# Two memory projections between the last turns of the query and key items of a hybrid decoder step

## The reference, cut to what matters

```python
z = rms_norm(h) @ w_in                     # conv group B, C, h; q, k, v; indexer queries and key
q, k = rope(rms_norm(q)), rope(rms_norm(k))
sel = top_k(indexer_scores(qi, iw, ki))    # 256 keys per prompt token, 66 per sample token
att = softmax(q @ k[sel]) @ v[sel]
h  += concat(B * conv3(C * h), att) @ w_out
mk, mv = split(rms_norm(mem_prompt, g_mem_src) @ w_kv_mem)   # 256 memory rows; mk is normed per head
h  += softmax(q_mem @ mk) @ mv @ w_o_mem
h  += ffn(h)
```

## Time and profile before

| | |
|---|---|
| median of 3 runs | 1862.89 us (1860.01 to 1864.6) |
| profiled execution, its own time | 1859.77 us |
| its span | 1858.0 us |
| mean granted TensorE clock | 0.954 |
| first key item on PE | 379.5 us |
| last turn of a key item | 452.5 us |
| scores of sample 0 | 462.1 us |
| prompt attention starts | 574.3 us |

### The profile page before, as it was taken

How to read it: one execution, slowest core, us unless ns; L and a number is a source line. 1 busy time by engine, 2 the same in 40 slices (tenths; PEclk the granted TensorE clock), 3 DMA queues, 4 the chain that set the end, 5 groups by cost and what they waited for, 6 DMA issues and landing times.

```text
span 1858.0 us, 33731 instructions
## 1 busy us (share of the span) xinstructions
PE 1719.4 (93%) x13725; PEld 1192.3 (64%) x13803; DVE 1113.3 (60%) x1901; ACT 810.9 (44%) x1475; POOL 735.1 (40%) x705
## 2 busy tenths in 40 slices
PE   6999999996787889989979997999999999999998
PEld 4543445443454655444568544888888888898998
DVE  5865665786797865456655237878888787300000
ACT  5465578744544864432355316544444444110100
POOL 3132266886540210320033416666666666401200
PEclk9998999997887999999978998999999999999999
DMA  7031112022424110301254112112121122321211
GB/s 229 17 104 51 35 35 85 30 74 90 155 76 137 53 47 1 111 1 35 89 155 140 62 40 91 46 53 63 46 69 47 47 69 86 97 95 39 94 36 29
DMA packets 136548, 132.75 MB, mean 71 GB/s; under 512 B 15358, under 2 KB 109630, under 8 KB 136356
## 3 DMA queue, kind: packets, MB, share of 16 engines
q1 hardware_dynamic: 123850, 118.79, 20.7%
q10 hardware_dynamic: 12544, 11.80, 2.0%
HBM read 114.58 MB, written 15.98 MB: 70 GB/s over the span
## 4 chain that ended last, share of the span: by engine, by line
PE 69%; DVE 15%; ACT 6%; issue 4%; POOL 3%; DMA 2%; SPq 1%; ACTq 0%; DVEq 0%; POOLq 0%
PE PS L1542 23%; PE PS L1599 5%; PE PS L1601 5%; PE PS L1600 5%; PE PS L938 4%; PE PS L939 4%; PE PS L940 4%; ACT arena L1674 2%; ACT arena L1615 2%; PE PS L1099 2%; PE PS L1097 2%; PE PS L1098 2%; PE PS L1244 1%; PE PS L1256 1%; POOL arena L2942 1%
## 5 line engine op out<-in xcount | busy, mean ns | idle before, releaser
L1542 PE MATMUL PS<-arena 128*128 128x272 f16 (+1 forms) x3696 | 430.6, 280 | 5.3 <-issue 5.3
L1542 PEld LDWEIGHTS PS<-arena 128*128 128x128 f16 (+1 forms) x3696 | 362.5, 98 | 73.4 <-issue 5.5
L1615 ACT ACTIVATE arena<-PS 128x512 f16<-128x512 f32 (+13 forms) x380 | 189.6, 530 | 229.4 <-PE PS L940 79.8
L1615 ACT ACTIVATE arena<-arena 128x512 f16<-128x512 f32 (+5 forms) x214 | 136.1, 657 | 235.9 <-PE PS L1542 116.4
L938 PE MATMUL PS<-arena 128*128 128x512 f16 (+3 forms) x648 | 227.9, 361 | 6.7 <-POOL arena L367 2.6
L367 POOL TENSOR_TENSOR arena<-arena 128x512 bf16<-128x512 f32 (+2 forms) x144 | 159.5, 1143 | 184.7 <-ACT arena L358 184.4
L939 PE MATMUL PS<-arena 128*128 128x512 f16 (+3 forms) x648 | 227.6, 361 | 0.0
L1599 PE MATMUL PS<-arena 128*128 128x256 f16 (+1 forms) x792 | 216.0, 273 | 1.4 <-POOL arena L916 1.0
L1601 PE MATMUL PS<-arena 128*128 128x256 bf16 (+1 forms) x792 | 215.9, 273 | 0.0
L1600 PE MATMUL PS<-arena 128*128 128x256 f16 (+1 forms) x792 | 215.9, 273 | 0.0
L940 PE MATMUL PS<-arena 128*128 128x512 bf16 (+2 forms) x609 | 212.6, 360 | 0.0
(11 more groups left out here) (351 smaller groups left out, 3713.7 us busy)
## 6 DMA issues: line engine op xcount, KB each, us to landing
arena<-w_gu SPq DMA_DIRECT2D x44, 512.0 KB, 4.8
arena<-w_down SPq DMA_DIRECT2D x8, 1408.0 KB, 7.6
arena<-w_in SPq DMA_DIRECT2D x8, 1024.0 KB, 5.5
arena<-w_kv_mem SPq DMA_DIRECT2D x8, 1024.0 KB, 5.3
arena<-cache_mem_k SPq DMA_DIRECT2D x32, 256.0 KB, 3.5
arena<-cache_mem_v ACTq DMA_DIRECT2D x28, 256.0 KB, 4.0
arena<-w_in SPq DMA_DIRECT2D x24, 256.0 KB, 3.9
arena<-x_prompt SPq DMA_DIRECT2D x9, 512.0 KB, 7.4
```

Source lines behind the costliest of these rows:

```text
L1542: mm = e.matmul(PS[:, product_bank(f, i) + c, 0:TC], w[:, i, k], s[i][:, q, c, :], start=first, stop=last)
L1615: e.activation(out, in_, ACT.Copy, **kw).then_inc(sem(name), 1)
```

## The change

Projections 0 and 1 of the memory leave the loop over samples and go between the last turns of the items: `memory_part(0, 0, 4)` behind the projection of item 35, then `(0, 4, 8)`, `(1, 0, 5)` and `(1, 5, 8)` in the three iterations after it, each in front of a turn. Projections 2 to 7 run one iteration sooner, `memory_part(b + 1)` in iterations 1 to 6. For that the row tiles are turned and split in items 27 and 31 in place of 29 and 35 (DVE's low parts behind items 28 and 32, before 30 and 37), chunk 1 is loaded behind the sixth key store, POOL splits it in front of the first value page (the other chunks stay where they were), the transposes of the conv state move from bank 7 to bank 5 and in front of the last turn, ACT evacuates projection b in iteration b, POOL's memset of `qm_all` moves behind the last rotation, and DVE's last update in the item loop from item 34 to item 35.

```diff
@@ sync @@
             B.load(e, 0)
-            store_roped(A_K)
+            store_roped(A_K, range(6))
             B.load(e, 1)
+            store_roped(A_K, range(6, NT))
@@ tensor @@
+            def memory_part(it, first, end):
...
             for L in range(NI1, NI + TURN_LAG):
-                if L == NI1 + 11:
+                if L == NI1 + 9:
                     NM.pe_turn(e, 0, lambda j: memx[:, j, :])
-                if L == NI1 + 17:
+                if L == NI1 + 13:
                     e.wait_ge(sem("nm_lo"), upto("nm_lo", 1))
                     NM.pe_turn(e, 1, lambda j: memx[:, j, :])
...
                 if L < NI:
                     project_item(L)
+                if L == NI - 1:
+                    e.wait_ge(sem("nm_lo"), upto("nm_lo", 2))
+                    memory_part(0, 0, 4)
+                if L == NI:
+                    memory_part(0, 4, KT)
+                if L == NI + 1:
+                    memory_part(1, 0, 5)
+                if L == NI + 2:
+                    e.wait_ge(sem("s2_raw"), NI)
+                    e.wait_ge(sem("s2_gn"), upto("s2_gn", 2 * NT))
+                    e.wait_ge(sem("conv_lo"), NC_T)
+                    for f in range(NC_T):
+                        t = e.transpose(PS[0:18, 5, f * P:(f + 1) * P], u_state[:, f, :], ident[:, :])
+                    t.then_inc(sem("mixst_tp"), 1)
+                    memory_part(1, 5, KT)
                 if L - TURN_LAG >= NI1:
                     turn_item(L - TURN_LAG)
...
             for b in range(DEC_B + 2):
+                part = 1 <= b < DEC_B - 1
                 if b < DEC_B:
-                    memory_part(b, 0, 3 if b else 5)
+                    if part:
+                        memory_part(b + 1, 0, 3)
...
-                    memory_part(b, 3 if b else 5, 6)
+                    if part:
+                        memory_part(b + 1, 3, 6)
                 if 1 <= b <= DEC_B:
                     sample_turn_probs(b - 1)
-                if b < DEC_B:
-                    memory_part(b, 6, KT)
+                if part:
+                    memory_part(b + 1, 6, KT)
@@ scalar @@
-                if L in (NI1 + 11, NI1 + 18):
-                    NM.act_hi(e, int(L == NI1 + 18))
+                if L in (NI1 + 9, NI1 + 13):
+                    NM.act_hi(e, int(L == NI1 + 13))
...
+            memory_out(0)
             for b in range(DEC_B + 1):
-                if b >= 1:
-                    memory_out(b - 1)
+                if 1 <= b < DEC_B:
+                    memory_out(b)
@@ vector @@
-                    if (L - NI1) % 2 == 0 and NI1 < L < NI - 1:
+                    if (L - NI1) % 2 == 0 and NI1 < L < NI - 2 or L == NI - 1:
                         update()
...
-                if L in (NI1 + 12, NI1 + 19):
-                    NM.dve_lo(e, int(L == NI1 + 19))
+                if L in (NI1 + 10, NI1 + 14):
+                    NM.dve_lo(e, int(L == NI1 + 14))
@@ gpsimd @@
-                if L == NI - 1:
-
-                    e.wait_ge(sem("s2_mm"), NI)
-                    e.memset(qm_all[:, :], 0.0).then_inc(sem("q_ht"), 1)
...
+            e.wait_ge(sem("s2_mm"), NI)
+            e.memset(qm_all[:, :], 0.0).then_inc(sem("q_ht"), 1)
...
+            e.wait_ge(sem("q_ht"), 5)
+            B.split_lo(e, 1)
             for b in range(DEC_B):
...
-                if b in (0, 2, 4):
+                if b in (2, 4):
                     B.split_lo(e, b // 2 + 1)
```

More of the change, by code:

```diff
@@ L1100, in _ @@
                 mm.then_inc(sem("s4_mm"), 1)
+            def memory_part(it, first, end):
+                c, j = it // 2, it % 2
+                if first == 0:
+                    if j == 0:
+                        B.ready(e, B_KV + c)
+                    if it >= 2:
+                        e.wait_ge(sem("mkv_ev"), it - 1)
+                out, wh, wl = PS[:, 6 + it % 2, :], B.high(c), B.low(c)
+                for k in range(first, end):
+                    e.matmul(out, xm_hi[j][:, k, :], wh[:, k, :], start=(k == 0), stop=False)
+                    e.matmul(out, xm_lo[j][:, k, :], wh[:, k, :], start=False, stop=False)
+                    mm = e.matmul(out, xm_hi[j][:, k, :], wl[:, k, :], start=False, stop=(k == KT - 1))
+                if end == KT:
+                    mm.then_inc(sem("mkv_mm"), 1)
             for L in range(NI1, NI + TURN_LAG):
-                if L == NI1 + 11:
+                if L == NI1 + 9:
                     NM.pe_turn(e, 0, lambda j: memx[:, j, :])
-                if L == NI1 + 17:
+                if L == NI1 + 13:
                     e.wait_ge(sem("nm_lo"), upto("nm_lo", 1))
@@ L1115, in _ @@
                     project_item(L)
+                if L == NI - 1:
[13 more added lines that the diff above has]
+                    memory_part(1, 5, KT)
                 if L - TURN_LAG >= NI1:
                     turn_item(L - TURN_LAG)
-            e.wait_ge(sem("s2_raw"), NI)
-            e.wait_ge(sem("s2_gn"), upto("s2_gn", 2 * NT))
-            e.wait_ge(sem("nm_lo"), upto("nm_lo", 2))
             e.wait_ge(sem("s4_ev"), len(L4))
@@ L1124, in _ @@
             e.wait_ge(sem("s2_lo"), split_items(NI))
[L1125 to L1128, removed]
             def sample_scores(b):
@@ L1160, in sample_values @@
                 e.wait_ge(sem("sv_lo"), upto("sv_lo", 2 * b + 2))
+                if b == 0:
+                    e.wait_ge(sem("mixst_ev"), 1)
                 for p, c in [(p, c) for p in range(4) for c in ((2, 0, 1) if p % 2 else (0, 1, 2))]:
@@ L1170, in sample_values @@
                 mm.then_inc(sem("sv_used"), 1)
[L1173 to L1189, removed]
             def turn_memory_heads(q):
@@ L1785, in _ @@
             e.wait_ge(sem("mixst_tp"), 1)
-            copy(mixst[:, :], PS[0:18, 7, :], "mixst_ev")
+            copy(mixst[:, :], PS[0:18, 5, :], "mixst_ev")
             def memory_out(it):
```

## The result

The changed kernel takes 1873.09 us (median of three runs, 1872.67 to 1874.1), the kernel before 1862.89. The ratio is 1.0058, with a 95% interval of 1.0035 to 1.0081: slower by 0.6%, by 10.2 us. The profiled execution took 1873.09 us, its span is 1871.3.

What follows compares the result with a forecast made beforehand. DVE's selection work was taken as the bound from sample 2 on, with PE waiting. Sum: −7.5 at scores 0, −4.4 at exp 2, +0.9 at maximum 3, +7.2 at maximum 5; 1862.9 + 7.2 = 1870 us, range 1858 to 1874.5.

Steps and rivals of the forecast that it cites:

- Row tiles: Key items: item 0 starts 2 to 3 us later, hidden; second tile's low part enters DVE's chain, +1.2 us.
- The moved update: DVE's bit search update behind the last norm, beside POOL's last rotation: still 4.4 us; last rotation ends 1.6 us sooner.
- Two projections at full clock: Projections 0 and 1 among the last turns: 48 matmuls take 10.5 us at full clock, PE through at about 451.
- late turns: Rival, slower: parts among the turns run at the low clock, PE through near 461, 1875 us; chance 0.10.
- c_sel: Before scores of sample 0: c_sel lands near 454, its wait to 462.07 goes, scores start near 454.5, 7.5 us sooner.
- What is late next: ACT holds exp 0 to 462.3, 5.4 us sooner; chunk 2's transfer holds exp 2 to 486.7, against 491.05.
- the lead: Time won by the sample iterations: 7.5 us at scores 0, 4.4 us left at exp 2.
- The first new wait: Iteration 3: PE waits for POOL's split of chunk 2 before its scores; maximum 3 at 507.0 against 506.16, +0.9 us.
- The second: Iteration 5: PE waits for chunk 3's split, 17.1 us from maximum 4; DVE idles 6.3 us, +7.2 at maximum 5.
- Nothing behind it gives anything back: After maximum 5: DVE's order is fixed and the attention follows, so the 6.3 us of idle time stay lost.
- the splits are hidden: Rival, faster: chunks 2 and 3 ready in time, lead of 4.4 to 7.5 us stays, 1855.4 to 1858.5; chance 0.12.

Runs made afterwards that it cites:

- run 4: Kernel before with only the memory row tiles turned and split at their sooner places: 1863.93 us, ratio 0.9992 to 1.0014.
- run 7: Run 2's kernel with DVE's update of the bit search back in front of the last norm (item 34): 1856.95 us.
- run 1: The changed kernel, unaltered, timed again beside the kernel before: 1872.19 us, ratio 1.0039 to 1.0065.
- run 2: Changed kernel with POOL's splits of chunks 2 and 3 in front of the value pages of samples 2 and 4, not behind: 1853.76 us.
- run 3: Changed kernel with memory projections 2 to 7 back in their own sample iterations on PE and ACT: 1860.44 us.
- run 9: Changed kernel with POOL's split of chunk 2 alone sooner, in front of the value page of sample 2: 1862.13 us.
- run 10: Changed kernel with POOL's split of chunk 3 alone sooner, in front of the value page of sample 4: 1863.11 us.
- run 8: Run 2's kernel with ACT's sign step in front of its high parts of chunk 2: 1853.86 us.
- run 6: Run 2's kernel with SP's order of before, chunk 1 loaded behind all key stores and in front of c_sel: 1857.84 us.
- run 5: Kernel before with only POOL's splits of chunks 2 and 3 moved in front of the value pages of samples 2 and 4: 1856.71 us.

## Why the prediction was right

The forecast was 1870 us, slower, in a range of 1858 to 1874.5; it is 1873.1. With the 2.07 us of chance taken out, step by step:

- *Row tiles.* +1.2 forecast, +1.1 in run 4; key item 0 later by 5.2 us and not by 2 to 3, but hidden, as said.
- *The moved update.* It took 447.06 to 452.14, 5.1 us, between the 4.4 of the earlier trace rows that was chosen and the 6.4 beside a split. The row was the nearer of the two. Still the lock shows in the 0.7 us on top of it: three of its short operations took 1.16, 0.64 and 0.65 us beside the rotation's instructions of 0.72 and 1.26, and 0.17 is what they take alone. The scores of sample 0 did not wait for it, but for POOL; run 7 puts the worth of the move at 1.5 to the attention, forecast 1.6.
- *Two projections at full clock.* Granted clock 1.00 from 437 to 453 us, as forecast; late turns did not happen.
- *c_sel.* Its wait is gone. The scores of sample 0 were forecast 7.5 us sooner; their start came 6.8 sooner (34.7 us behind the zero before, 28.0 after), their end only 5.1. **This term was mis-sized.** The start waited for POOL's copies, which end at 456.91, and the scores then ran at the low clock, which was not in the sum: 3.82 us up to maximum 0, where they took 2.14 before. Windows of the changed kernel, the scores, and of before:

```profile
457.38:461.20 3.82, 3.82 (x26) 2.92 (x27) 0.00 (x0) 3.82 (x5) 3.27 (x3) 0.50 0.39 137
```

```profile
462.07:464.20 2.13, 2.13 (x26) 1.86 (x27) 0.00 (x0) 2.13 (x4) 0.00 (x0) 1.00 0.07 23
```

- *What is late next.* ACT held exp 0 and the transfer of chunk 2 held exp 2, as said; 3.5 us of the lead were left at exp 2 (489.57 − 429.42 against 491.05 − 427.35), forecast 4.4.
- *The first new wait.* Maximum 3 was forecast at +0.9 and came at +0.8. DVE's idle time before it was 3.05 and not 5, since its own work had grown: the split stood beside more of its short operations. The prediction did not see that the split is a load on DVE too. It hit this number all the same, because PE's wait, which ended later, covered it. There is luck in it too: the lead at exp 2 was 0.9 us short, and from exp 2 to maximum 3 it took 19.5 us where the forecast had 20.35 (13.8, 3.95 and 2.6); the two misses cancel.
- *The second.* From maximum 4 to the end of the split 17.1 us, as forecast (523.35 to 540.43). POOL's timeline of the changed kernel, as in the earlier trace rows:

```profile
528.80 11.63 POOL L367 TENSOR_TENSOR arena<-arena 128x512 bf16<-128x512 f32 x8
```

  DVE idled for 5.81 us (forecast 6.3), maximum 5 came at +6.6 (forecast +7.2), the attention at +7.3.
- *Nothing behind it gives anything back.* True of the stretch to the attention. Whether more was lost behind it is open. The medians differ by 10.2 us, and in run 1 by 9.3, where the stretch to the attention has 7.3 and 7.2; runs 2, 3, 9 and 10 also gain 2.8 to 3.9 us more in the medians than in that stretch, but all four are set against the one median of run 1. From the attention's start to the end of the span it is 1280.8 us before, 1284.7 and 1281.6 in the two traces of the changed kernel, and 1279.1 to 1284.5 in the other eleven, whose programs have the same work there. The clock is no clear mark either. From 610 to 630 us the changed kernel's is 0.89 and then 0.83, and in run 1 0.83 twice, where the kernel before and run 2 have 1.00 in the same part of the attention:

```profile
610.00:620.00 10.00, 8.26 (x116) 6.49 (x112) 6.03 (x10) 8.12 (x11) 1.81 (x2) 0.89 0.01 2
620.00:630.00 10.00, 7.93 (x103) 5.51 (x103) 7.72 (x15) 6.77 (x14) 7.15 (x7) 0.83 0.44 150
```

  But runs 3, 9 and 10 have one such stretch as well, and run 8 has none and still takes 1283.2 us from the attention's start. The cause of these 2 to 3 us stays open; the forecast had no term for them.

Of the rivals, *the splits are hidden* would have needed chunk 2 low by 495.2 us on the clock of before, 497.3 here; it was low at 503.16. Run 2 is this rival made true, and it gave more than the lead.

## What to carry to other kernels

Work that is moved sooner brings its inputs' due times with it: moving the consumer one iteration without its producer turned two short waits into 15 us each. To price a producer's place on GpSimd, count the short VectorE operations that will stand beside it, about one GpSimd instruction of delay for each here, and put it beside a wait of VectorE; that took 5.5 us off VectorE's own operations in the kernel before, with nothing else changed. And a lead won early is worth only what no fixed wait behind it takes back: SP's order gave 4 us in run 6 once the two waits were gone.

## What was not expected of the hardware

- Short VectorE operations, six values wide, went from 0.17 to 1.08 us beside GpSimd instructions of 1.12 us, those with a single tensor input (L2410, TENSOR_SCALAR) like those with two (L2411). An operation 1024 wide lost 0.84 us, about as much, but less in proportion: 2.11 in place of 1.27.
- TensorE was granted the low level, 0.50 (1.2 GHz), for the whole of the scores of sample 0, after it had run at the full one (2.4 GHz) from 437 to 453 us and then had 0.46 us of work in the 4.3 up to them. Before, it had 6.6 us of work in the 12 up to them, the first projection's among it, and they were granted 1.00 and took 2.14 us in place of 3.8. It is no chance of one trace: in the three kernels that keep the first projection in front of these scores (before, runs 4 and 5) they took 2.14, in the eleven traces of those that moved it 3.60 to 3.82. So a group of matmuls taken out of a pause made the next group dearer here.
